# A fused two-model block kernel: opening reordered, semaphores raised and cleared by several engines, squares piled, row fetches with a bounds check

## The reference, cut to what matters

```python
mod = jax.nn.silu(c) @ ada_w[l] + ada_b[l]          # shifts, scales, gates: 6 pieces of 1024
h = rmsnorm(x, g) * (1 + scale) + shift             # ahead of every mixer and feed-forward
...
def hier_moe(xt, ...):                              # xt: 512 tokens in layer 0 (latent and context), 256 in layer 1
    g_idx = argmax(xt @ wg + bg); top_p, top_e = top_k(softmax(expert logits of that group), 2)
    ...                                             # tokens sorted by expert
    hb = jax.nn.silu(xb @ w1[e]) * (xb @ w3[e])
    y = hb @ w2[e]
    return sum over a token's two experts of weight * y
```

## Time and profile before

| | us |
|---|---|
| median of 3 runs | 2893.27 |
| lowest and highest | 2891.22 and 2893.32 |
| profiled execution, its own time | 2896.54 |
| its span in the profile | 2894.6 |
| granted TensorE clock, mean over the span | 0.99 |
| TensorE busy | 2756.4 (95%) |
| VectorE busy | 1116.9 (39%) |
| ScalarE busy | 704.1 (24%) |
| GpSimd busy | 27.2 (1%) |
| DMA, mean over the span | 232 GB/s |

### The profile page before, as it was taken

The page is one execution under the profiler, slowest core; times in us unless marked ns, Lnnn a source line. Parts: engine busy times, 40 slices in busy tenths (PEclk is TensorE's granted clock), DMA queues, the critical chain, the costliest instruction groups (busy, mean ns, idle before and its releaser), DMA issues. The chain is left out here.

```text
span 2894.6 us, 33661 instructions
## 1 busy us (share of the span) xinstructions
PE 2756.4 (95%) x12386; PEld 1543.0 (53%) x12386; DVE 1116.9 (39%) x2471; ACT 704.1 (24%) x1339; POOL 27.2 (1%) x34
## 2 busy tenths in 40 slices
PE   6999999999999998999989999999979999999998
PEld 3555444444467777888554433333347765444444
DVE  2342477771146665771342422222233332112222
ACT  1343200000045553000252222212122222222222
POOL 0000000000000000000000000000000000000000
PEclk9999999999999999999999999999999999999999
DMA  6133456552221213885004699999944337999995
GB/s 258 75 117 117 174 221 240 235 217 73 103 101 61 71 59 117 305 311 191 33 15 196 256 421 421 421 421 422 422 162 144 131 135 296 421 422 422 422 422 233
DMA packets 104133, 671.79 MB, mean 232 GB/s; under 512 B 10865, under 2 KB 19313, under 8 KB 27377
## 3 DMA queue, kind: packets, MB, share of 16 engines
q1 hardware_dynamic: 98720, 651.25, 56.5%
q0 software_dynamic: 3600, 13.11, 1.2%
q10 hardware_dynamic: 1728, 6.29, 0.5%
HBM read 663.27 MB, written 7.34 MB: 232 GB/s over the span
## 5 line engine op out<-in xcount | busy, mean ns | idle before, releaser
L637 PE MATMUL PB<-A,RING 128*128 128x512 f32 (+1 forms) x1408 | 454.6, 486 | 2.7 <-ACT A L514 2.7
L637 PEld LDWEIGHTS PB<-A,RING 128*128 128x128 f32 x1408 | 267.3, 190 | 190.4 <-issue 167.5
L409 DVE SCALAR_TENSOR_TENSOR WORK<-RING,MORE 128x1024 f32<-128x1024 f32 x288 | 335.6, 1222 | 21.7 <-ACT MORE L651 12.2
L463 PE MATMUL PB<-BIG,RING 128*128 (+2 forms) x928 | 312.4, 499 | 5.7 <-PEq L605 3.3
L463 PEld LDWEIGHTS PB<-BIG,RING 128*128 128x128 f32 x928 | 176.5, 191 | 140.5 <-issue 129.9
L2463 DVE TENSOR_TENSOR BIG<-BIG,PB 64x512 f32<-64x512 f32 x32 | 22.1, 690 | 363.6 <-ACT BIG L2363 363.6
L2926 DVE TENSOR_TENSOR BIG<-BIG,PB 64x512 f32<-64x512 f32 x32 | 22.1, 690 | 348.8 <-ACT BIG L2844 348.8
L529 DVE SCALAR_TENSOR_TENSOR X<-PB,MODS,X 128x256 f32<-128x256 f32 x72 | 32.5, 480 | 299.3 <-PE PB L491 298.6
L656 ACT ACTIVATE RS<-PB 128x512 f32<-128x512 f32 (+1 forms) x44 | 21.6, 491 | 417.0 <-PE PB L637 417.0
L2246 PE MATMUL PB<-RING,BIG 128*64 128x512 f32 x512 | 117.0, 593 | 2.4 <-DMA RING<-moe_w 1.8
L1650 PE MATMUL PB<-A,RING 128*128 128x512 f32 x256 | 112.3, 592 | 1.0 <-ACT A L514 1.0
(11 more groups left out here) (465 smaller groups left out, 4038.3 us busy)
## 6 DMA issues: line engine op xcount, KB each, us to landing
RING<-moe_w SPq DMA_DIRECT2D x160, 1024.0 KB, 13.5
RING<-ada_rows SPq DMA_DIRECT2D x72, 1024.0 KB, 6.8
RING<-ffn_w SPq DMA_DIRECT2D x66, 1024.0 KB, 4.8
SPARE<-moe_w SPq DMA_DIRECT2D x64, 1024.0 KB, 11.9
CST<-moe_w SPq DMA_DIRECT2D x32, 1024.0 KB
RS<-moe_w SPq DMA_DIRECT2D x32, 1024.0 KB
MORE<-moe_w SPq DMA_DIRECT2D x32, 1024.0 KB, 16.5
A<-moe_w SPq DMA_DIRECT2D x32, 1024.0 KB
```

The source lines that it names most:

```text
L409: dve_.scalar_tensor_tensor(out=JUNK[:, n % 4, :], in0=RING[:, s, b * D:(b + 1) * D], scalar=1.0, in1=WIDE[:, side // 2, w, :], op0=ALU.mu ...
L463: last = pe_.matmul(PB[:, m, 0:tp], tile(s, 2, D)[:, r, m * P:(m + 1) * P], src(2 * i + r), start=first and r == 0, stop=False)
L637: last = pe_.matmul(PB[:, 2 * s + j, 0:t], tile(s, KD, P, j * KD * P)[:, k, :], A[:, k, 0:t], start=k == 0, stop=k == KD - 1)
```

## The change

- The block at the start is gone. `raise_share` brings a third of the signals each to 8, on GpSimd, TensorE and VectorE, at the head of the opening's own block; SP and ScalarE start with their work at once.
- SP's order in the opening: X, the constants, the condition vectors, chunks 0, 2, 1, V, the first quarter of mla_w_in, chunk 3, the other three quarters, the heads, the late constants.
- TensorE takes the chunks in the order 0, 2, 1, 3 and turns them in banks 5, 6, 7, 0. Slices 0 to 3 of A are finished after chunks 0 and 2, slices 4 to 7 after 1 and 3. Of each four slices VectorE now takes the latent half and the last slice's context half, ScalarE three context halves. ScalarE loads its root table ahead. Two fillers instead of three.
- The token numbers and row bases are stored less 1024, and 1024 is added back when they become an index, so that an empty slot has the index 1024. The indirect transfers get a bound (511 for the fetches, 1023 for the returns) and don't count an index beyond it as an error; such a row isn't to be copied.
- After the last turn of the mixture VectorE adds the squares of slices 1 to 3 into slice 0; TensorE sums slices 4 to 7 and the pile, five products instead of eight.
- The clearing block is shared by the five engines, 10 or 11 semaphores each.
- A boundary without a product has six fillers instead of three (only the odd mixer's).

```diff
+AWAY = 1024.0
-    put("row_base", np.tile(np.where(e % 4 < 2, (e // 4 * 2 + e % 4) * CAP, 0), (P, 1)))
+    put("row_base", np.tile(np.where(e % 4 < 2, (e // 4 * 2 + e % 4) * CAP, 0) - AWAY, (P, 1)))
-    put("token", p[:, None] + P * np.arange(NT)[None, :])
+    put("token", p[:, None] + P * np.arange(NT)[None, :] - AWAY)
...
-    with nc.Block() as block:
-        @block.sync
-        def _(sp):
-            for s in signals.values():
-                sp.sem_inc(s.sem, FIRST)
+    def raise_share(eng, n):
+
+        for s in list(signals.values())[n::3]:
+            eng.sem_inc(s.sem, FIRST)
...
+        order, flip_banks = (0, 2, 1, 3), (5, 6, 7, 0)
...
-                sp.dma_start(CS[:].rearrange("p a b c -> p (a b c)"), io["cvec"]).then_inc(sig("cvec_in").sem, 16)
-                sp.dma_start(CST[:, 0:late], io["consts"]).then_inc(sig("consts_in").sem, 16)
...
-                for c in range(4):
-                    for a in range(2):
-                        sp.dma_start(spot(2 * c + a), ada_of(0)[c, a]).then_inc(sig(f"chunk_in{c}").sem, 16)
+                sp.dma_start(CST[:, 0:late], io["consts"]).then_inc(sig("consts_in").sem, 16)
+                sp.dma_start(CS[:].rearrange("p a b c -> p (a b c)"), io["cvec"]).then_inc(sig("cvec_in").sem, 16)
+                for c in order[:3]:
+                    chunk(c)
                 sp.dma_start(V[:], io["vecs"]).then_inc(sig("inputs_in").sem, 16)
-                early(sp)
+                latent_weights(sp, 0)
+                chunk(order[3])
+                for j in range(1, 4):
+                    latent_weights(sp, j)
+                head_weights(sp)
...
+            @block.gpsimd
+            def _(pool):
+                raise_share(pool, 0)
+
             @block.tensor
             def _(pe):
+                raise_share(pe, 1)
...
-                for c in range(4):
+                for n, c in enumerate(order):
+                    if n == 3:
+                        turn_over(2)
                     pe.wait_ge(sig(f"chunk_in{c}").sem, sig(f"chunk_in{c}").at(32))
                     for a in range(2):
                         last = chunk_products(1 + c, 0, a, spot(2 * c + a))
                     last.then_inc(sig("chunk_made").sem, 1)
-                    if c:
-                        turn_over(c - 1)
+                    if n in (1, 2):
+                        turn_over(n - 1)
                 turn_over(3)
-                keep_warm(1, 3)
+                keep_warm(1, 2)
...
+                act_.activation(SMALL[:, 639:640], con("eps"), ACT.Sqrt)
...
+                for n in range(3):
+                    drain(n)
+                shift(0)
+                drain(3)
+                shift(1)
...
+                raise_share(dve, 2)
...
+                for n in range(2):
+                    for j in range(2):
+                        c = order[2 * n + j]
+                        dve.wait_ge(sig("mod_flipped").sem, sig("mod_flipped").at(2 * n + j + 1))
+                        chain(dve_.tensor_tensor(MODS[:, 0, 4 * c:4 * c + 4, :],
...
+                    for k, w in [(k, 0) for k in range(4 * n, 4 * n + 4)] + [(4 * n + 3, 1)]:
+                        last = dve_.tensor_scalar(A[:, k, half(w)], A[:, k, half(w)], GAIN[:, w, k:k + 1],
+                                                  piece(0, 0, k, w), ALU.mult, ALU.add)
...
             else:
-                keep_warm(6, 3)
+                keep_warm(6, 6)
...
                     nc.gpsimd.indirect_dma_start(XG[:, b, :], None, token_rows,
-                                                 bass.IndirectOffsetOnAxis(INDEX[b][:], 0)).then_inc(rows_in[b].sem, 16)
+                                                 bass.IndirectOffsetOnAxis(INDEX[b][:], 0),
+                                                 bounds_check=T - 1, oob_is_err=False).then_inc(rows_in[b].sem, 16)
...
-                                bass.IndirectOffsetOnAxis(RETURN[c * nt + a][:], 0)).then_inc(rows_back[a].sem, 16)
+                                bass.IndirectOffsetOnAxis(RETURN[c * nt + a][:], 0),
+                                bounds_check=NE // 2 * CAP - 1, oob_is_err=False).then_inc(rows_back[a].sem, 16)
...
-                for k in range(KD):
-                    pe.wait_ge(sig("squared").sem, sig("squared").at(k + 1))
-                    last = pe_.matmul(PB[:, 0, 0:t], ONES, WORK[:, k * T:k * T + t], start=k == 0, stop=k == KD - 1)
+                for k in (4, 5, 6, 7, 0):
+                    if k:
+                        pe.wait_ge(sig("squared").sem, sig("squared").at(k + 1))
+                    else:
+                        pe.wait_ge(sig("piled").sem, sig("piled").at(3))
+                    last = pe_.matmul(PB[:, 0, :], ONES, WORK[:, k * T:(k + 1) * T], start=k == 4, stop=k == 0)
...
-                    dve_.tensor_scalar(INDEX[b][:], PB[:, 3, T - 2:T - 1], 0.25, None, ALU.add) \
+                    dve_.tensor_scalar(INDEX[b][:], PB[:, 3, T - 2:T - 1], AWAY + 0.25, None, ALU.add) \
...
+                for k in range(1, 4):
+                    dve.wait_ge(sig("squared").sem, sig("squared").at(k + 1))
+                    dve.wait_ge(sig("piled").sem, sig("piled").at(k - 1))
+                    dve_.tensor_tensor(WORK[:, 0:T], WORK[:, 0:T], WORK[:, k * T:(k + 1) * T], ALU.add) \
+                        .then_inc(sig("piled").sem, 1)
...
+        def start_over(eng, n):
+
+            for s in counted[n::5]:
+                eng.sem_clear(s.sem)
+                eng.sem_inc(s.sem, FIRST)
+
         with nc.Block() as block:
             @block.sync
             def _(sp):
-                for s in counted:
-                    sp.sem_clear(s.sem)
-                    sp.sem_inc(s.sem, FIRST)
+                start_over(sp, 0)
+
+            @block.tensor
+            def _(pe):
+                start_over(pe, 1)
...
-    opening(mla_early)
+    opening(mla_latents, mla_heads)
```

More of the change, by code:

```diff
@@ L271, in chunk_flips, with opening @@
         return last
-    def opening(early):
+    def opening(latent_weights, head_weights):
         def spot(n):
@@ L287, in _, with chunk @@
             def _(sp):
[L288 to L289 removed]
+                def chunk(c):
+                    for a in range(2):
+                        sp.dma_start(spot(2 * c + a), ada_of(0)[c, a]).then_inc(sig(f"chunk_in{c}").sem, 16)
                 for w, name in enumerate(("xT", "ctxT")):
@@ L356, in _ @@
                 dve.wait_ge(sig("inputs_in").sem, sig("inputs_in").at(16))
-                dve.wait_ge(sig("mod_flipped").sem, sig("mod_flipped").at(4))
-                chain(dve_.tensor_tensor(MODS[:, 0, 0:16, :], PB[:, 5, 0:32].rearrange("p (n w) -> p n w", w=2),
-                                         vec("ada_b", 0, 16).unsqueeze(2).broadcast_to([P, 16, 2]), ALU.add))
-                for w in range(2):
-                    last = dve_.scalar_tensor_tensor(
-                        out=GAIN[:, w, :], in0=MODS[:, 0, KD:2 * KD, w], scalar=1.0, in1=vec("norm1", 0, KD),
-                        op0=ALU.add, op1=ALU.mult)
@@ L708, in build, with mla_latents, mla_heads @@
     IN_COLS, HALF_COLS = KD * MLA_IN, 2 * T + 2 * T + 3 * T + 3 * S
-    def mla_early(sp):
-        for j in range(4):
-            c = slice(j * IN_COLS // 4, (j + 1) * IN_COLS // 4)
-            sp.dma_start(RINGF[:, c], io["mla_w_in"][:, c]).then_inc(loaded[0].sem, 16)
+    def mla_latents(sp, j):
+        c = slice(j * IN_COLS // 4, (j + 1) * IN_COLS // 4)
+        sp.dma_start(RINGF[:, c], io["mla_w_in"][:, c]).then_inc(loaded[0].sem, 16)
+    def mla_heads(sp):
         for c in (slice(0, HALF_COLS // 2), slice(HALF_COLS // 2, HALF_COLS)):
@@ L2488, in places_back @@
                         for a in range(nt):
-                            last = dve_.tensor_scalar(RETURN[n * nt + a][:], PLACE[:, n, a:a + 1], 0.25, None, ALU.add)
+                            last = dve_.tensor_scalar(RETURN[n * nt + a][:], PLACE[:, n, a:a + 1], AWAY + 0.25, None, ALU.add)
                     last.then_inc(sig("placed").sem, 1)
@@ L2571, in _ @@
             def _(sp):
-                for s in counted:
-                    sp.sem_clear(s.sem)
-                    sp.sem_inc(s.sem, FIRST)
+                start_over(sp, 0)
+            @block.tensor
+            def _(pe):
+                start_over(pe, 1)
+            @block.scalar
+            def _(act):
+                start_over(act, 2)
+            @block.vector
+            def _(dve):
+                start_over(dve, 3)
+            @block.gpsimd
+            def _(pool):
+                start_over(pool, 4)
         for s in counted:
```

46 lines of the change are left out of this document (26 added, 20 removed).

## The result

The changed kernel takes 2871.09 us, the median of 4 runs (2869.84 to 2873.42), beside 2893.30 (2891.22 to 2895.43, 4 runs) of the kernel before: a ratio of 0.9918 [0.9906, 0.9931], the medians 22.2 us apart. The ratio isn't the quotient of the two medians: it would make 23.7 us. The forecast was 2869.8.

A forecast was written before the change was run, and what follows sets the result against it. Bounds: TensorE, busy 95% of the span, and DMA at about 421 GB/s in the expert stages. Gains of 8.0 + 9.5 + 1.0 + 2.6 + 2.4 = 23.5 us from 2893.27 gave 2869.8, range 2860 to 2882.

The forecast's parts named there:

- Opening: Kernel start: latents begin 9.1 us earlier, less 1.1 for the half clock; 8.0 us gained (6 to 9.4).
- products 2.4 us, as from 42.24 to 44.65: Opening, behind the fourth chunk: TensorE's products were to take 2.4 us, as in the kernel before.
- Skipping: First expert stage: fetches and returns skip empty slots; 9.5 us gained, between 5.5 and 13.4, outer end 0.
- The estimate of 8.7, by the busiest engine: Expert stage: the busiest DMA engine skips 37 of 112 rows, mean 64; 8.7 us with the returns.
- at 63.4 B holds: Sign in the expert stage: late turns staying at 63.4 us, not 62.2 to 62.8, would mean skipping moves no time.
- B: Rival for the expert stage: skipping moves no time, only 13.0 us is gained, total 2880.3; chance 0.17.
- Return rows: Expert stage's tail: shorter waits for returned rows, 1.0 us (0 to 1.6); low clock, up to 2 us, not counted.
- Squares: Tail of the expert stage: five ones-products instead of eight, 2.6 us gained; the piling adds hidden behind TensorE.
- Clearing: Block after the expert stage: clearing shared by five engines takes 1.6 us instead of 4.0; 2.4 gained (1.4 to 3.2).
- A: Rival for the expert stage: the skip is worth its full mean, 13.4 us, total 2865.9; chance 0.18.
- C: Rival for the opening: it gives half, through unready queues or slow raises; 4 us less gain, total 2873.8; chance 0.10.
- D: Rival for the returns: the bounds check slows GpSimd's eight issues; at 5 us more each, total 2909.8; chance 0.03.

The follow-up runs named there:

- e10: The changed kernel unaltered, measured and profiled again: 2867.37 us (4 runs), ratio to the kernel before 0.9911.
- e5: The kernel before with only its semaphore raising shared by PE, VectorE and POOL, old transfer order kept: 2885.89 us (6 runs), ratio 0.9972.
- e1: The changed kernel without the bounds and the offset of 1024, so every row is fetched and returned: 2877.89 us (1 run).
- e3: The changed kernel with filled slots packed so one DMA engine's eight slots fill first; returned rows not the tokens' own: 2872.37 us (1 run).
- e9: The changed kernel with three fillers before chunk 3, chunk 3 ahead of mla_w_in, slots in steps of 9, unequal clearing shares: 2858.97 us, ratio to before 0.9879.
- e8: The changed kernel with eight ones-products, clearing by SP alone and three fillers before the odd mixer, as before: 2869.59 us (1 run).
- e2: The changed kernel with ranks laid into the 64 slots in steps of 9, spreading the filled ones: 2870.48 us (4 runs), ratio to before 0.9917.
- e6: The kernel before with only the row skipping added (bounds and offset of 1024): 2883.93 us (7 runs), ratio 0.9961.
- e4: The changed kernel with five more fillers ahead of the opening's wait for chunk 3: 2866.51 us (4 runs), ratio to before 0.9906.
- e7: The changed kernel with three fillers ahead of chunk 3, and chunk 3 before mla_w_in's first quarter: 2865.16 us (4 runs), ratio to before 0.9900.

## Why the prediction was right, and where it was not

The total was 1.3 us off and the direction and the mechanisms held, but four terms of the sum were mis-sized and happened to cancel, so the closeness is in part luck. The same kernel's repeat, e10, was 2.4 us under the forecast.

- **Opening, 8.0 foreseen, 7.1 measured** (8.1 to 9.7 in the other five profiles of the same opening)**.** The transfers came as worked out, to 0.5 us at each chunk. The step that failed is "products 2.4 us, as from 42.24 to 44.65": it took the wait of 2.07 us as the pattern for one that had become 4.52. Before, the clock fell behind the wait; now it had fallen inside it, so the two sets of products took 3.6 us at 1.2 GHz and the modulation was out at 42.0 instead of 40.8. The 1.1 us of clock were charged to the latents alone. Those cost 0.8: the clock came back about 1.6 us behind their start, near the 2.2 foreseen (the row's 0.57 puts the rise before at 53.7, not 53.3, and 11.5 us behind 35.9 is 47.4). That held in this profile; in the other five the clock was back before the latents began. And the reordering, which the sum didn't price apart, earned nothing over the shared raise (e5).
- **Skipping, 9.5 foreseen, 6.9 measured** (8.1 in e10)**.** The reason for a value under 13.4, the parts with the low slots, is what e1 to e3 show. The middle of 5.5 and 13.4 was still too high by 2.6. The estimate of 8.7, by the busiest engine, is nearer. The step that failed: both put 5.5 or more on the sixteenth and seventeenth fetch and the returns, which relieve the queue only behind the sixteenth fetch. TensorE waited 2.72 for a weight there, and 2.1 to 3.5 came. The sign "at 63.4 B holds" failed too: one turn took 63.41 while rows were skipped, because its fullest group had no empty slot.
- **Return rows, 1.0 foreseen, 4.5 measured.** The waits of 1.6 went (1.9). The other 2.6 is the half clock that set in under them, which the text named as "up to 2 us, not counted". It should have been read: a stretch at 0.50 of nearly 7 us starts inside that wait in the trace of before.
- **Squares, 2.6 and 2.6.** The pile is done 0.2 us before its first product starts, as worked out.
- **Clearing, 2.4 foreseen, 2.0 measured.** "0.8 at SP's 0.037, 2.6 at three times that" was the right pair of bounds; TensorE and VectorE lie near the upper one. From the changed kernel to e9 they did 10 and 8 operations fewer and drained 0.8 and 0.9 earlier, counted from the memset (+6.4 and +6.3 to +5.6 and +5.4): some 0.1 us each.
- **Fillers, 0 and 0** (e8).

Of the rivals, A (the mean share) falls by e2 and e3, which skip as many rows and earn 6.7 and 1.5. B (nothing moves) falls by e6. C (half an opening) falls: 7.1 came, though the clock took a part. D (a slow check) would have needed 2.9 us more an issue; it took 0.05.

## What to carry to other kernels

Take serial semaphore work off the engine that issues the first transfer: that one edit gave 7.4 to 8.1 us here (e5), and a reordering on top gave nothing that could be told from the spread. Put fillers into a wait of some us that can't be shortened: ten short ones brought the latents 1.5 to 3.6 us forward (e4). Where rows of an indirect transfer are skipped, lay the filled ones out evenly over the partitions: with the same bytes, three layouts saved 1.5, 4.9 and 6.7 us. Price a wait of TensorE together with the half clock that it can bring on, and price small parts from marks in several traces rather than from one run's time.

## What the runs showed of the hardware that was not expected

- A skipped row moves no bytes (13.11 to 6.07 MB) but still counts as a packet (3600 in both), and the bounds check costs GpSimd 0.05 us an issue of 128 rows.
- How much a skipped row saves depends on the slot it is in.
- TensorE and VectorE need about 0.1 us for a clear or a raise. SP took 0.037 when it cleared alone and about 0.08 with four engines doing the same (the step from 11 to 16 semaphores, e9); why wasn't tried.
- The clock fell inside a wait of 4.52 us and rose at different times in six executions of the same opening: 0.97 in 40 to 42 in one, 0.50 until about 47.5 in another, worth 2 us. What decides between the two is open. With TensorE busy through that wait it didn't fall in any of the three kernels that did so (e4, e7, e9). In the old order a wait of 2.07 us was enough: the clock fell inside it in e6 and behind it in the kernel before and e5.
